# Two waits of TensorE for its own sums behind a layer norm, left out

## The chip, the cores and the metric

The kernel runs on one core of one Trainium2 chip. The metric is the device time of one execution in microseconds. Three runs of the kernel before took 1831.89, 1832.02 and 1832.16 us; the median is 1832.02 us.

## The reference, cut to what matters

One decoder block over 16 meta tokens and 256 tokens of width 2048, in float32: a half-step SwiGLU feed-forward (inner width 5632), a token mixer, a second half-step feed-forward and a last RMS norm. The mixer makes one input projection, runs a gated short convolution on one half of its channels and a 31-tap convolution with a layer norm on the other, and ends in one output projection:

```
y_sc = b_sc * causal_dwconv(c_sc * v_sc, conv_sc_w)
z = a_cf * sigmoid(g_cf)
z = causal_dwconv(z, conv_cf_w) + conv_cf_b
y_cf = silu(layernorm(z, ln_cf_g, ln_cf_b))      # mean and variance over 1024 channels
h = concatenate([y_sc, y_cf], -1) @ w_out
```

The layer norm takes its mean and variance over the channels. The channels lie on the 128 partitions in 8 tiles, so each of the two statistics needs a sum over the tiles (VectorE) and then a sum over the partitions (TensorE, a product with a matrix of ones).

## The kernel before, in words

Activations lie transposed, channels on partitions and tokens along the free axis. Every float32 operand is split into a high part (written by ScalarE) and a low part (written by VectorE), and each 128x128 weight tile makes three products: high times high (line 591), high times low (592) and low times high (593). The last stage uses lines 717 to 719 for the same three.

The weights come in 640 blocks of 512 KB, in an order written out by hand, the same on all engines. For each block SyncE starts the transfer into one of four raw buffers (line 446) once the low part of the block four before is made; ScalarE writes the high part (line 845) once the transfer has landed and TensorE has used the block four before; VectorE writes the low part (line 1135); TensorE waits for it (`start_block`) and makes the block's 24 products. The stages are gu1, down1, ag, cv, b, out_sc, out_cf, gu2 and down2. Each engine's queue is in order, and between blocks it has the other work of the stage.

The change lies in out_sc, the first half of the output projection: 4 groups of 4 blocks, counted b = 0 to 15, then out_cf with b = 16 to 31. Group 0 and 2 accumulate in PSUM banks 0 to 3, group 1 and 3 in banks 4 to 7, each in columns 0 to 255 of its banks. The layer norm runs in the shadow of these blocks:

- VectorE finishes the last taps of the convolution and the sum over the 8 tiles, and splits it into `sum_hi` and `sum_lo`.
- After block 6 TensorE sums them over the partitions, two products with a matrix of ones (lines 606 and 607), into columns 256 to 511 of bank 0: `layernorm_sums`.
- VectorE, after it has made the low part of block 8, waits for that sum, scales it (`ln_mu`, line 1446) and centres the 8 tiles; ScalarE squares them (line 998), VectorE adds the squares up (lines 1453 to 1457) and splits the sum (1150, 1152). Then comes the low part of block 11.
- After block 10 TensorE sums over the partitions again, into columns 256 to 511 of bank 4; VectorE reads it (line 1462), makes the reciprocal root, normalizes, and writes the low parts of the layer norm's output, which out_cf reads from block 16 on.

After each sum TensorE has two kinds of wait: one for the sum's own end (`ln_mean_done`, `ln_var_done`) right behind it, and, one block later (b = 7 and b = 11), one for VectorE's having read it (`ln_mu_set`, `ln_var`), before the next group begins in those banks. TensorE waits for its own end at four more places: behind the sums of the three RMS norms (`square_sums`), and before out_sc's first block, for the end of the stage b.

Of the kernel before, what the change touches and what calls it, by code (L numbers as in the profile page):

```python
# [39 lines left out]
def build(nc, x, meta_tokens, ffn1_norm, ffn1_w_gate, ffn1_w_up, ffn1_w_down, mix_norm, w_in, b_in,  # L40
# [45 lines left out]
    with ExitStack() as ctx:  # L86
# [3 lines left out]
        def sem(name):  # L90
            return ctx.enter_context(nc.semaphore(name))
# [205 lines left out]
        ln_mean_done, ln_mu_set, centred = sem("ln_mean_done"), sem("ln_mu_set"), sem("centred")  # L297
        ln_sq, ln_var_sum, ln_var_done = sem("ln_sq"), sem("ln_var_sum"), sem("ln_var_done")
# [27 lines left out]
        def banks_before(phase, g):  # L326

            return KD + SET * group0[phase] + SET * g
# [214 lines left out]
        def _(pe):  # L543
# [60 lines left out]
            def sum_over_partitions(dst, toks):  # L604

                pe.matmul(dst, ones_r[:, :], sum_hi[:, toks], start=True, stop=False)
                return pe.matmul(dst, ones_r[:, :], sum_lo[:, toks], start=False, stop=True)  # L607
# [189 lines left out]
            def layernorm_sums(b):  # L797


                if b == 6:  # L800
                    pe.wait_ge(sum_low, nth_sum["ln_mean"])
                    pe.wait_ge(emptied, banks_before("out_sc", 1))
                    sum_over_partitions(ps[:, 0, SEQ:2 * SEQ], slice(0, SEQ)).then_inc(ln_mean_done, 1)
                    pe.wait_ge(ln_mean_done, 1)
                if b == 10:
                    pe.wait_ge(sum_low, nth_sum["ln_var"])
                    pe.wait_ge(emptied, banks_before("out_sc", 2))
                    sum_over_partitions(ps[:, SET, SEQ:2 * SEQ], slice(0, SEQ)).then_inc(ln_var_done, 1)
                    pe.wait_ge(ln_var_done, 1)

                if b == 7:
                    pe.wait_ge(ln_mu_set, 1)
                if b == 11:
                    pe.wait_ge(ln_var, 1)
# [9 lines left out]
            for g in range(G_D):  # L824
                single_group("out_sc", g, g % 2, y_hi, y_lo, 0, slice(0, SEQ), KS,
                             ysc_lo, lambda i: i + 1, layernorm_sums)
# [840 lines left out]
```

## Time and profile before

| | |
|---|---|
| median of three runs | 1832.02 us |
| the profiled execution | 1831.56 us |
| its span | 1829.7 us |
| TensorE products busy | 1819.4 us, 99% |
| VectorE busy | 1190.7 us, 65% |
| ScalarE busy | 932.6 us, 51% |
| mean granted TensorE clock | 0.999 |

The span is the time from the first to the last instruction; 1831.56 - 1829.7 = 1.86 us of the profiled execution lie around it. PE is TensorE's products, PEld its weight loads, DVE is VectorE, ACT ScalarE, SP SyncE. Busy PE includes products that overlap, so 99% says that one product at least was under way. The chain of waits is followed backwards from the last instruction, at each step to what released it.

### The profile page before, as it was taken

What the parts mean: (1) busy time and instruction counts of PE and PEld (TensorE: products, weight loads), DVE (VectorE), ACT (ScalarE), POOL (GpSimd) and SP (SyncE); (2) the same over time, 40 slices, a digit from 0 to 9 for tenths busy, and PEclk for the clock granted to TensorE, in tenths of its full rate; (3) what the DMA queues carried; (4) which work ended last, traced back from release to release, by engine and by line L of the source; (5) the groups of instructions that cost most, each with busy time, mean ns of one, the idle gap of its engine ahead of it and who ended that gap; (6) DMA issues with size and microseconds to landing.
All of it is one profiled execution on the core that took longest, in us unless ns stands there. A gap on an engine that the chain in (4) does not pass through costs nothing.

```text
span 1829.7 us, 34627 instructions
## 1 busy us (share of the span) xinstructions
PE 1819.4 (99%) x14327; PEld 1778.0 (97%) x14327; DVE 1190.7 (65%) x1383; ACT 932.6 (51%) x1181; POOL 5.5 (0%) x15
## 2 busy tenths in 40 slices
PE   9999999999999999999999999999999999999998
PEld 9999999999999999999999999999999999988886
DVE  7555555555554544468899997755555565588897
ACT  7434343444433443349988776444444444455554
POOL 1000000000000000000000000000000000000000
PEclk9999999999999999999999999999999999999999
DMA  7655555555567777756556565966666666677665
GB/s 236 192 177 175 181 174 181 173 180 175 177 176 177 179 178 179 177 168 190 178 185 189 170 207 183 239 207 190 193 192 195 195 191 191 193 225 240 197 209 164
DMA packets 301845, 346.53 MB, mean 189 GB/s; under 512 B 27711, under 2 KB 241057, under 8 KB 301760
## 3 DMA queue, kind: packets, MB, share of 16 engines
q1 hardware_dynamic: 283104, 340.44, 62.1%
q10 hardware_dynamic: 18368, 4.73, 1.3%
q8 instruction: 58, 0.95, 0.2%
q14 instruction: 27, 0.22, 0.0%
q0 software_dynamic: 288, 0.19, 0.0%
HBM read 341.11 MB, written 4.19 MB: 189 GB/s over the span
## 4 chain that ended last, share of the span: by engine, by line
PE 98%; DVE 1%; ACT 0%; DMA 0%; issue 0%; SPq 0%; DVEq 0%; ACTq 0%
PE ps L591 29%; PE ps L593 29%; PE ps L592 29%; PE ps L718 4%; PE ps L717 4%; PE ps L719 4%; DMA m_rows<-in_meta_tokens 0%; DVE w_same__lo L1135 0%; PE ps L553 0%; DVE o_tok L1348 0%; ACT sq_tok L868 0%; DVE o_tok L1627 0%; DVE o_tok L1371 0%; DVE partial L1342 0%; PE ps L622 0%
## 5 line engine op out<-in xcount | busy, mean ns | idle before, releaser
L593 PE MATMUL ps<-x_hi,w_class__lo 128*128 128x272 f32 (+2 forms) x3200 | 901.6, 282 | 0.0
L591 PE MATMUL ps<-x_hi,w_class__hi 128*128 128x272 f32 (+2 forms) x3200 | 900.8, 281 | 0.1
L592 PE MATMUL ps<-x_lo,w_class__hi 128*128 128x272 f32 (+2 forms) x3200 | 900.3, 281 | 0.0
L1135 DVE TENSOR_TENSOR w_class__lo<-raw,w_class__hi 128x1024 fp32r<-128x1024 f32 x400 | 489.2, 1224 | 402.8 <-ACT w_class__hi L845 401.3
L845 ACT ACTIVATE w_class__hi<-raw 128x1024 fp32r<-128x1024 f32 x400 | 424.1, 1061 | 558.5 <-PE ps L593 558.2
L592 PEld LDWEIGHTS ps<-x_lo,w_class__hi 128*128 128x128 f32 x3200 | 602.2, 188 | 0.0
L591 PEld LDWEIGHTS ps<-x_hi,w_class__hi 128*128 128x128 f32 x3200 | 601.5, 188 | 0.3 <-PE ps L607 0.3
L593 PEld LDWEIGHTS ps<-x_hi,w_class__lo 128*128 128x128 f32 x3200 | 601.5, 188 | 0.0
L845 ACT ACTIVATE w_same__hi<-raw 128x1024 fp32r<-128x1024 f32 x200 | 210.9, 1059 | 261.0 <-PE ps L593 172.4
L1135 DVE TENSOR_TENSOR w_same__lo<-raw,w_same__hi 128x1024 fp32r<-128x1024 f32 x200 | 241.3, 1222 | 144.6 <-ACT w_same__hi L845 144.3
L593 PE MATMUL ps<-a_hi,w_same__lo 128*128 128x272 f32 x640 | 183.4, 287 | 0.0
L591 PE MATMUL ps<-a_hi,w_same__hi 128*128 128x272 f32 x640 | 183.4, 287 | 0.0
L592 PE MATMUL ps<-a_lo,w_same__hi 128*128 128x272 f32 x640 | 183.3, 286 | 0.0
L592 PEld LDWEIGHTS ps<-a_lo,w_same__hi 128*128 128x128 f32 x640 | 120.6, 188 | 0.0
L591 PEld LDWEIGHTS ps<-a_hi,w_same__hi 128*128 128x128 f32 x640 | 120.5, 188 | 0.0
L593 PEld LDWEIGHTS ps<-a_hi,w_same__lo 128*128 128x128 f32 x640 | 120.5, 188 | 0.0
L718 PE MATMUL ps<-w_same__hi,a_both 128*128 128x512 f32 x262 | 101.9, 389 | 0.0
L717 PE MATMUL ps<-w_same__hi,a_both 128*128 128x512 f32 x262 | 101.9, 389 | 0.0
L719 PE MATMUL ps<-w_same__lo,a_both 128*128 128x512 f32 x262 | 101.9, 389 | 0.0
L990 ACT ACTIVATE tap_product<-z,par 128x256 f32<-128x256 f32 x232 | 98.8, 494 | 0.0
L591 PE MATMUL ps<-y_both,w_same__hi 128*128 128x256 f32 x256 | 71.0, 277 | 0.2
L592 PE MATMUL ps<-y_both,w_same__hi 128*128 128x256 f32 x256 | 70.7, 276 | 0.0
(204 smaller groups left out, 1705.5 us busy)
## 6 DMA issues: line engine op xcount, KB each, us to landing
raw<-in_ffn_w_up SPq DMA_DIRECT2D x176, 512.0 KB, 3.5
raw<-in_ffn_w_down SPq DMA_DIRECT2D x176, 512.0 KB, 5.1
raw<-in_ffn_w_gate SPq DMA_DIRECT2D x175, 512.0 KB, 3.5
raw<-in_w_in SPq DMA_DIRECT2D x80, 512.0 KB, 3.6
raw<-in_w_out SPq DMA_DIRECT2D x32, 512.0 KB, 4.8
x_tok<-in_x SPq DMA_DIRECT2D x4, 512.0 KB, 7.8
out_y<-res ACTq DMA_DIRECT2D x32, 64.0 KB, 4.1
o_tok<-out_y ACTq DMA_DIRECT2D x8, 256.0 KB, 5.6
```

The lines of the kernel that those rows point to most:

```text
L591: pe.matmul(dst, w_high, act_high, start=first, stop=False)
L592: pe.matmul(dst, w_high, act_low, start=False, stop=False)
L593: return pe.matmul(dst, w_low, act_high, start=False, stop=last)
L717: pe.matmul(dst, act_high, w_high, start=begins, stop=False)
L718: pe.matmul(dst, act_low, w_high, start=False, stop=False)
L719: return pe.matmul(dst, act_high, w_low, start=False, stop=ends)
L845: act.activation(block_weights(phase, g, i)[0], raw_rows(phase, s), ACT.Copy).then_inc(hi_ready, 1)
L990: act.activation(tap_product[:, q % PRODUCTS, c % 2, :], z[:, c, 2 + n:2 + n + SEQ], ACT.Copy, scale=cf_tap(2 + n, c)).then_inc(cf_product, 1)
L1135: dve.tensor_tensor(w_lo, raw_rows(phase, s), w_hi.bitcast(F32), ALU.subtract).then_inc(lo_ready, 1)
```

## The change

TensorE's waits for the end of its own two sums are left out. Nothing else is changed: VectorE still waits on `ln_mean_done` and `ln_var_done` before it reads the sums, and TensorE still waits one block later until VectorE has read them.

```diff
@@ -801,12 +801,10 @@
                     pe.wait_ge(sum_low, nth_sum["ln_mean"])
                     pe.wait_ge(emptied, banks_before("out_sc", 1))
                     sum_over_partitions(ps[:, 0, SEQ:2 * SEQ], slice(0, SEQ)).then_inc(ln_mean_done, 1)
-                    pe.wait_ge(ln_mean_done, 1)
                 if b == 10:
                     pe.wait_ge(sum_low, nth_sum["ln_var"])
                     pe.wait_ge(emptied, banks_before("out_sc", 2))
                     sum_over_partitions(ps[:, SET, SEQ:2 * SEQ], slice(0, SEQ)).then_inc(ln_var_done, 1)
-                    pe.wait_ge(ln_var_done, 1)
```

## Rows read from the trace of the kernel before

**Rows 1.** The page, parts 1, 2 and 4: busy times, clock in tenths, chain by engine
```profile
PE 1819.4 (99%) x14327; PEld 1778.0 (97%) x14327; DVE 1190.7 (65%) x1383; ACT 932.6 (51%) x1181; POOL 5.5 (0%) x15
...
PEclk9999999999999999999999999999999999999999
...
PE 98%; DVE 1%; ACT 0%; DMA 0%; issue 0%; SPq 0%; DVEq 0%; ACTq 0%
```

**Rows 2.** The waits of the weight loads, whole run: line waited for, total, times, longest
```profile
PEld ps L591 <- PE ps L607: 1.3, 5, 0.3
...
PEld ps L591 <- PE ps L593: 0.3, 1, 0.3
```

**Rows 3.** Timeline of PE around the mean's sum: start us, duration, line, operands
```profile
1043.00 0.28 PE L591 MATMUL ps<-y_both,w_same__hi 128*128 128x256 f32 x1
...
1045.72 0.28 PE L606 MATMUL ps<-sum_hi,ones_r 128*128 128x256 f32 x1
1045.84 0.28 PE L607 MATMUL ps<-sum_lo,ones_r 128*128 128x256 f32 x1
1046.18 0.39 PE L591 MATMUL ps<-y_both,w_same__hi 128*128 128x256 f32 x1
1046.40 0.28 PE L592 MATMUL ps<-y_both,w_same__hi 128*128 128x256 f32 x1
...
1047.10 0.28 PE L592 MATMUL ps<-y_both,w_same__hi 128*128 128x256 f32 x1
```

**Rows 4.** Timeline of the weight loads around the mean's sum; idle before one in brackets
```profile
1045.72 0.19 PEld L607 LDWEIGHTS ps<-sum_lo,ones_r 128*128 128x128 f32 x1
1046.17 0.19 PEld L591 LDWEIGHTS ps<-y_both,w_same__hi 128*128 128x128 f32 x1 [0.26 <-PE ps L607]
```

**Rows 5.** Timeline of PE around the variance's sum
```profile
1057.31 0.28 PE L607 MATMUL ps<-sum_lo,ones_r 128*128 128x256 f32 x1
1057.64 0.39 PE L591 MATMUL ps<-y_both,w_same__hi 128*128 128x256 f32 x1
1057.87 0.28 PE L592 MATMUL ps<-y_both,w_same__hi 128*128 128x256 f32 x1
...
1058.57 0.28 PE L592 MATMUL ps<-y_both,w_same__hi 128*128 128x256 f32 x1
```

**Rows 6.** Timeline of PE where the stage out_sc begins
```profile
1026.21 0.28 PE L593 MATMUL ps<-x_hi,w_kept__lo 128*128 128x256 f32 x1
1026.55 0.39 PE L591 MATMUL ps<-y_both,w_same__hi 128*128 128x256 f32 x1
```

**Rows 7.** Timeline of DVE beside the two sums
```profile
1046.16 0.42 DVE L1446 TENSOR_SCALAR ln_mu<-ps 128x256 f32<-128x256 f32 x1 [2.18 <-PE ps L607]
...
1055.19 0.43 DVE L1152 TENSOR_TENSOR sum_lo<-ln_sum,sum_hi 128x256 fp32r<-128x256 f32 x1
1055.53 1.22 DVE L1135 TENSOR_TENSOR w_same__lo<-raw,w_same__hi 128x1024 fp32r<-128x1024 f32 x1
1057.62 0.42 DVE L1462 TENSOR_SCALAR step<-ps 128x256 f32<-128x256 f32 x1 [0.87 <-PE ps L607]
```

**Rows 8.** Timeline of DVE before out_cf's second block
```profile
1071.74 2.36 DVE L1135 TENSOR_TENSOR w_same__lo<-raw,w_same__hi 128x1024 fp32r<-128x1024 f32 x2
```

**Rows 9.** Timeline of PE where the second block of out_cf begins
```profile
1074.09 0.28 PE L591 MATMUL ps<-y_both,w_same__hi 128*128 128x256 f32 x1
```

**Rows 10.** The chain that ended last, its last stretch: start us, us, what
```profile
1804.94 0.24 PE ps L719
...
1805.20 0.02 ACT partial L915
```

**Rows 11.** Timeline of ACT near the end
```profile
1808.28 1.06 ACT L845 ACTIVATE w_same__hi<-raw 128x1024 fp32r<-128x1024 f32 x1 [0.58 <-DMA raw<-in_ffn_w_down]
```

**Rows 12.** Timeline of DVE near the end
```profile
1811.58 2.35 DVE L1135 TENSOR_TENSOR w_same__lo<-raw,w_same__hi 128x1024 fp32r<-128x1024 f32 x2
```

**Rows 13.** The weight tiles' transfers, 1040 to 1800 us: time to landing
```profile
DMA to landing us min/median/max: 3.3/4.2/7.7
```

## The prediction, made before the change was run

> **What bounds the kernel now.** I read four views. First the page: PE is busy 99% of a span of 1829.7 us, its granted clock is 0.9 or more of full speed in all 40 slices, and the chain that ended last is PE for 98% of the span [rows 1]. So nearly every nanosecond in which TensorE stands still is in the span, and VectorE and ScalarE matter only where they make it stand still. Second, the waits of the weight loads. Apart from the first 10 us there are two lines: five waits for line 607, 1.3 us in total, and one of 0.3 us for line 593 [rows 2]. The five are the sums over the partitions, each followed by a wait for its own end; the change removes two of them, so this view prices the idle time at 2 x 1.3 / 5 = 0.52 us. Third, the timeline around the two sums, because idle time is not the whole price (below). Fourth, the last stretch of the chain, to see whether a gain at 1046 us reaches the end.
>
> **The two waits, step by step.** The undisturbed spacing comes from block 6: its first product starts at 1043.00 and line 606, 24 products later, at 1045.72 [rows 3], so 2.72 / 24 = 0.113 us a product. Behind the sum's second product (1045.84) the next should start at 1045.95; it starts at 1046.18, lasts 0.39 instead of 0.28, and the one behind it starts 0.22 later, at 1046.40 [rows 3]. The weight load shows why: loads and products normally run side by side, one load ahead; here the load of block 7 stood idle for 0.26 us, until the sum had ended, and starts at 1046.17, with its product [rows 4]. So three things are paid: the end of the sum (0.34 - 0.113 = 0.23 us), one load that nothing hides (0.22 - 0.113 = 0.11 us), and slightly wide spacings for the next few products. Together: from line 607 at 1045.84 to the eighth product of block 7 at 1047.10 are 1.26 us for 8 spacings; 8 x 0.1133 = 0.907; the wait costs 0.35 us. At the variance: 1057.31 to 1058.57, again 1.26 us, again 0.35 [rows 5]. Of another kind of work the same wait costs the same: before out_sc TensorE waits for the end of line 593, with 1026.55 - 1026.21 = 0.34 us to the next product [rows 6].
>
> What comes back in their place? Block 7 and block 11 still wait for their low part. At an ordinary block border that wait shows no widening (1045.72 is one spacing behind block 6, and the two lines of [rows 2] are all the waits there are), so its cost is nothing when the low part is early. Block 7's is long made: VectorE had been idle for 2.18 us before 1046.16 [rows 7]. I charge 0. Block 11's is close. VectorE starts it at 1055.53 and ends at 1055.53 + 1.22 = 1056.75 [rows 7]. Its start can't move forward with TensorE: it lies behind work that began with reading the mean at 1046.16, and the mean's sum itself starts no earlier than before. TensorE comes to block 11 0.35 us earlier from the first wait, and doesn't stand behind the second: its product would be at 1057.31 + 0.11 - 0.35 = 1057.07, the load one spacing ahead at 1056.96. That is 0.2 us after 1056.75. A handover from VectorE to TensorE is not among the rows; the nearest is from TensorE to its own load, 1045.84 + 0.28 = 1046.12 to 1046.17, 0.05 us [rows 3, 4]. So it is ready at about 1056.80, 0.15 us in time. I charge 0, and keep 0.2 us as the upper bound (late by a little, and then a load that nothing hides, 0.11).
>
> Sum: 0.353 + 0.353 = 0.71 us gained, 0 lost. The bounds from the rows are 0.52 (the idle time of the view of waits alone) and 0.74 (both starts are rounded to 0.01 us, and the last widened spacings may reach a product further).
>
> **Does it reach the end?** The variance's sum comes 0.35 us earlier (its operands are ready at 1055.19 + 0.43 = 1055.62 [rows 7], TensorE gets there at 1056.84), so VectorE's work behind it moves by 0.35 and TensorE by 0.71: VectorE's lead over TensorE shrinks by 0.36. The least lead that I find there is at out_cf's second block: its low part is the first of two that start at 1071.74 and take 2.36 together, so done at 1072.9 [rows 8]; its first product starts at 1074.09, the load at 1073.98 [rows 9]. A lead of 1.1 us becomes 0.7: no wait. At the end the last PE piece of the chain is line 719 at 1804.94, and ScalarE takes over at 1805.20, released by it [rows 10]; from there VectorE and ScalarE set the time, all counted from that release. So the last 25 us move as a whole. The transfers also hang on VectorE's low parts and move along.
>
> The Trainium skill bears on the size. "TensorE: Matmul & The Clock Gate", section Single matmul latency, gives (398 + N) / 2.4 ns for a lone product at full clock, and section Back-to-back issue gap gives N / 2.4 + 2.5 for a streamed one. For N = 256 that is 272 ns against 109 ns. The trace has 0.28 and 0.113 us for these two, so it agrees; the difference, 0.163 us each, would make 0.33 us for the two waits, 1831.7 on the median. It leaves out the unhidden load and the way from the semaphore to the load, which the timeline shows; the row decides. The same page (Step-by-step, part 1) has the next weights loaded while a product runs: that speaks for the load's 0.11 us coming back.
>
> **The own time and the median.** The profiled execution took 1831.56 us: span 1829.7, and 1.86 around it. The sum makes that 1829.0 and 1830.85. It stood 0.46 below the median of the three runs, 1832.02, so runs differ by more than the effect does. On the median: 1832.02 - 0.71 = 1831.31, said as 1831.3 us. A measurement of this kernel can tell about 0.2% from no change, 3.7 us; the whole effect is 0.04%.
>
> **The rivals.**
> (a) The low part of block 11 takes the place of the second wait. For it: the 0.15 us lead just worked out. Against it: the lead is positive. It would give back 0.05 to 0.2 us: 1831.4 to 1831.5.
> (b) Only the end of the sum is saved, and the first load of the next block still lies bare. For it: block 7's load had its own wait in both cases. Against it: ordinary borders have that wait and show no bare load. Gain 2 x 0.23 = 0.46: 1831.56.
> (c) The gain is absorbed before the end, or the diff does nothing because what holds TensorE there is something else. For it: the last 25 us of the chain are not PE. Against it: they start from a PE release, and the weight loads have no wait for another engine behind the start [rows 2]. 1832.0.
> (d) Slower: a transfer near the end. The high part that starts at 1808.28 had waited 0.58 us for its transfer [rows 11]; it ends at 1809.34, and its low part starts on VectorE at 1811.58 [rows 12], in the very stretch that sets the end: a lead of 2.24 us. Transfers land after 4.2 us in the median and 7.7 at most [rows 13]. If the new times make this one meet other traffic and go from the one to the other, it is 3.5 late, VectorE waits 3.5 - 2.24 = 1.3, and the result is 1.3 - 0.7 = 0.6 above before: 1832.6. It decides from 2.24 + 0.71 = 2.95 us of delay on. Against it: the transfers move along with their consumers, so nothing new meets.
>
> **Chances.** Forecast 0.68, (a) 0.12, (b) 0.05, (c) 0.11, (d) 0.04. The range takes the forecast with (a), (b) and most of (c), and leaves room for the scatter between executions, of which the 0.46 us above is the measure: 1830.8 to 1832.1 us. Faster by over 0.2%, which needs 3.7 us, has no case here: 0.02. Slower by as much: 0.02. Within 0.2%: 0.96.
>
> **What would show it.** The waits of the weight loads have three for line 607, 0.8 us in total, instead of five. In the timeline line 607 of the mean is followed by a product of block 7 after 0.11 us that lasts 0.28, and the same at the variance. Line 607 of the variance starts 0.35 us earlier, the last PE piece of the chain 0.71 earlier, and the span is 1829.0. Rival (a) shows as an idle load behind the variance's sum that waits for line 1135; (b) as a 0.39 us product; (c) as a new wait later on. The prediction is wrong if the span is above 1829.4 or if TensorE's part before 1804 us has not moved by 0.6 to 0.8 us.

## The result: slower by 2.6 us, and the profile after

| | before | after |
|---|---|---|
| median of 20 runs each | 1831.88 us (1831.46 to 1832.70) | 1834.47 us (1833.87 to 1835.13) |
| ratio | | 1.0014, 95% interval 1.0008 to 1.0020 |
| the profiled execution, its span | 1831.56, 1829.7 us | 1834.84, 1833.0 us |

The change cost 2.6 us where 0.7 us of gain was predicted. It is small, but the interval leaves out no change. The two waits are gone from the waits of the weight loads, to which [rows 2] had five and one:

```profile
PEld ps L591 <- PE ps L607: 0.8, 3, 0.3
...
PEld ps L591 <- PE ps L593: 0.3, 1, 0.3
```

So is the gap behind the mean's sum, in the timeline of PE that answers to [rows 3]:

```profile
1046.62 0.28 PE L606 MATMUL ps<-sum_hi,ones_r 128*128 128x256 f32 x1
1046.74 0.28 PE L607 MATMUL ps<-sum_lo,ones_r 128*128 128x256 f32 x1
1046.86 0.28 PE L591 MATMUL ps<-y_both,w_same__hi 128*128 128x256 f32 x1
1046.98 0.28 PE L592 MATMUL ps<-y_both,w_same__hi 128*128 128x256 f32 x1
1047.09 0.28 PE L593 MATMUL ps<-y_both,w_same__lo 128*128 128x256 f32 x1
```

Line 607 is followed after 0.12 us, and the product behind it lasts 0.28 us, not 0.39. All of this was predicted. But look at the spacings: 0.12, 0.12, 0.11, where block 6 had 0.113. One block later it is plain; this row is 24 products behind 1046.86:

```profile
1049.68 0.28 PE L591 MATMUL ps<-y_both,w_same__hi 128*128 128x256 f32 x1
```

(1049.68 - 1046.86) / 24 = 0.1175 us a product. Taken over whole blocks, from the exact starts in the trace, the spacing is 113.3 ns in all of out_sc, out_cf and gu2 before, and 117.8 ns after, from block 7 of out_sc to block 3 of gu2. Then comes the sum of gu2's norm with its wait, which is left in, and the spacing is 113.3 again. The view of busy time by stretches shows it as a count of products. Its columns are: the stretch, its length, the busy time and in brackets the number of instructions of PE, PEld, DVE, ACT and POOL, the granted clock, the DMA share, GB/s. The number behind PE is the count. Four stretches: out_sc's blocks before the mean's sum; between the two sums; behind the variance's sum up to gu2's; gu2. The kernel before:

```profile
1032.00:1044.00 12.00, 12.00 (x108) 12.00 (x107) 11.84 (x19) 7.31 (x10) 0.00 (x0) 1.00 0.55 177
1048.00:1056.00 8.00, 8.00 (x73) 8.00 (x72) 7.86 (x13) 5.19 (x5) 0.00 (x0) 1.00 0.47 150
1062.00:1122.00 60.00, 60.00 (x532) 60.00 (x531) 53.23 (x91) 42.34 (x68) 0.00 (x0) 1.00 0.65 204
1140.00:1200.00 60.00, 60.00 (x531) 60.00 (x531) 40.59 (x44) 27.07 (x29) 0.00 (x0) 1.00 0.90 236
```

The kernel after:

```profile
1032.00:1044.00 12.00, 12.00 (x108) 12.00 (x107) 11.86 (x20) 7.47 (x12) 0.00 (x0) 1.00 0.51 166
1048.00:1056.00 8.00, 8.00 (x70) 8.00 (x69) 7.90 (x11) 4.33 (x4) 0.00 (x0) 1.00 0.46 154
1062.00:1122.00 60.00, 60.00 (x512) 60.00 (x511) 51.56 (x86) 40.59 (x67) 0.00 (x0) 1.00 0.64 201
1140.00:1200.00 60.00, 60.00 (x531) 60.00 (x531) 42.30 (x48) 28.36 (x30) 0.00 (x0) 1.00 0.87 228
```

The first and the last stretch have the same count within one; between the sums 70 stand against 73, behind them 512 against 532: 60 us / 532 = 0.113, 60 / 512 = 0.117 (a product counts if it overlaps the stretch, so each count is two or three high). The granted clock is 1.00 in all eight lines, and in the two slow stretches VectorE and ScalarE are no busier than before, but for 0.04 us of VectorE in the second. TensorE is at work all the time in every stretch.

One view does show the pace without counting: the mean time of one instruction, by line. In 1062 to 1122 us a product has 276 ns before and 281 after, whichever its line. Among the weight loads every third is longer, that of line 593 (the last number before the idle time is the mean in ns; before, then after):

```profile
L593 PEld LDWEIGHTS ps<-y_both,w_same__lo 128*128 128x128 f32 x156 | 29.3, 188 | 0.0
```

```profile
L593 PEld LDWEIGHTS ps<-y_both,w_same__lo 128*128 128x128 f32 x158 | 30.3, 192 | 0.0
```

The loads of the other two lines have 188 ns in both. From the stage b on this holds in every trace: one load of three is longer wherever the pace is slow, and none where it is fast.

The size follows: 29 blocks of 24 products at 117.78 - 113.33 = 4.45 ns make 3.10 us; less the 0.71 us of the two waits, 2.39. It can be measured between the same two instructions, out_sc's first product and line 607 in gu2. Before, the first is in [rows 6] and the second is this:

```profile
1125.89 0.28 PE L607 MATMUL ps<-sum_lo,ones_r 128*128 128x256 f32 x1
```

After, they are these two:

```profile
1027.45 0.39 PE L591 MATMUL ps<-y_both,w_same__hi 128*128 128x256 f32 x1
```

```profile
1129.17 0.28 PE L607 MATMUL ps<-sum_lo,ones_r 128*128 128x256 f32 x1
```

Before 1125.89 - 1026.55 [rows 6] = 99.34 us, after 1129.17 - 1027.45 = 101.72: 2.38 more. The other 0.90 us by which this profile is longer lie before out_sc (1027.45 against 1026.55), in the first 10 us, where three profiles of the unchanged kernel differ by 0.7 us too. The medians differ by 2.6; the 0.2 beyond 2.4 are within what the executions scatter.

### The profile page after: what moved, and what is told of

The parts are those of the page before. It is cut to its first block, busy times and chain, and to the rows that moved or that the text cites. A ratio compares the mean times of both kernels' runs of the same rounds, so it can differ in the third digit from the quotient of the medians.

```text
span 1833.0 us, 34625 instructions
## 1 busy us (share of the span) xinstructions
PE 1823.0 (99%) x14327; PEld 1782.1 (97%) x14327; DVE 1190.5 (65%) x1383; ACT 932.5 (51%) x1181; POOL 5.5 (0%) x15
## 4 chain that ended last, share of the span: by engine, by line
PE 98%; DVE 1%; ACT 0%; issue 0%; DVEq 0%; ACTq 0%
PE ps L593 29%; PE ps L591 29%; PE ps L592 29%; PE ps L717 4%; PE ps L718 4%; PE ps L719 4%; PE ps L573 0%; PE ps L553 0%; DVE w_same__lo L1133 0%; DVE o_tok L1346 0%; ACT sq_tok L866 0%; DVE o_tok L1625 0%; DVE o_tok L1369 0%; DVE partial L1340 0%; PE ps L622 0%
```

## The experiments

Sixteen runs were made. Three of them repeat the two main kernels (e5, e12, e16), and three repeat the kernel of another run (e6, e14, e15). Where nothing else is said the base is the changed kernel. "Slow pace" is 117.8 ns a product, "fast pace" 113.3. Each group of runs was timed beside the kernel before on one chip: e1 to e8 on one, e9 to e12 on a second, e13 to e16 on a third.

One thing has to be known before the traces are compared. There are two kinds of execution, and they part long before out_sc, in code that no run changed. In both, TensorE waits for its own end behind the sum of gu1's norm, at 33 us. The first product behind that wait, in the kernel before and in e2:

```profile
33.02 0.39 PE L591 MATMUL ps<-x_hi,w_rows_hi 128*128 128x272 f32 x1
```

```profile
33.73 0.40 PE L591 MATMUL ps<-x_hi,w_rows_hi 128*128 128x272 f32 x1
```

By the exact times it lasts 394 ns in the first kind, and the next one starts 230 ns behind it; in the second kind it is 397 and 233 to 234 ns. At the next such sum, at 807 us, each trace has its own two numbers again, and behind the wait before out_sc the next product starts after 229 to 230 ns in the first kind, 221 to 222 in the second. Each of the 18 traces is clearly one or the other. The first kind are the two main profiles and e1, e3, e5, e6, e10, e12, e13, e15 and e16; the second are e2, e4, e7, e8, e9, e11 and e14. Each chip had both. With y at its own place, out_sc begins fast in all traces of the first kind and slow in all of the second. What makes an execution of the one kind or the other isn't known; by 33 us it is settled. So what an edit does is read from traces of one kind.

**One wait put back, and a wait put elsewhere.**

```diff
# e1: behind the mean's sum
+                    pe.wait_ge(ln_mean_done, 1)
# e2 and e6: behind the variance's sum instead
+                    pe.wait_ge(ln_var_done, 1)
# e3: behind block 7, and likewise behind block 11
                 if b == 7:
+                    pe.wait_ge(block_used, block0["out_sc"] + 8)
                     pe.wait_ge(ln_mu_set, 1)
```

> The changed kernel with the wait behind the mean's sum put back; only the one behind the variance's sum stays out. Theory (pace): once the products of a sum run on without a wait, every product behind them is issued 117.8 ns after the one before instead of 113.3, until TensorE's next wait for its own end. Then blocks 7 to 10 of out_sc keep 113.3 ns, and the 25 blocks from b = 11 to the sum in gu2 (600 products) take 4.5 ns more each: +2.7 us, less 0.35 for the wait, so 2.3 us above before, about 1834.2 us. Rival (neighbours): the slower products come from reads and writes of VectorE, ScalarE and the transfers that TensorE now meets at other moments; they would depend on the times, not on which wait is gone, so with half the shift the slow stretch should be partly gone from both places and the time lie between, 1832 to 1833.

Stretches two and three of e1:

```profile
1048.00:1056.00 8.00, 8.00 (x73) 8.00 (x72) 7.86 (x13) 4.87 (x4) 0.00 (x0) 1.00 0.50 154
1062.00:1122.00 60.00, 60.00 (x512) 60.00 (x511) 51.60 (x88) 40.40 (x68) 0.00 (x0) 1.00 0.64 202
```

73 products between the sums, 512 behind the second: the fast pace where the wait is, the slow one from where it is missing. Time: 1.0012 of the kernel before, interval 1.0002 to 1.0021, medians 1835.26 against 1833.28, 2.0 us. The theory had 2.3, and 2.31 us is what lies between the two traces from out_sc's first block to gu2's sum (the medians may mix the two kinds of execution: the profiled one took 1834.21 us, the nine others 1835.08 to 1835.90); the rival, which wanted a time between and both stretches partly slow, is out.

> The changed kernel with a wait of TensorE for its own end one block later, behind blocks 7 and 11, where it already waits for VectorE's having read the sum. Theory (pace): any wait for the own end resets the pace, wherever it stands: 117.8 ns in block 7 and in block 11, 113.3 in all others; the span about 0.2 us above before's (2 x 24 x 4.5 ns; the two waits cost what they cost before). Rival (the sum must be drained before the next product): the pace stays at 117.8 behind the later waits, since the sums themselves still run on.

```profile
1048.00:1056.00 8.00, 7.94 (x69) 7.74 (x68) 7.86 (x13) 5.13 (x5) 0.00 (x0) 1.00 0.46 150
1062.00:1122.00 60.00, 60.00 (x532) 60.00 (x531) 53.13 (x92) 42.08 (x68) 0.00 (x0) 1.00 0.65 205
```

e3 has 532 products again behind the second late wait; by blocks only 7 and 11 are slow (117.7), 8 to 10 and all from 12 on fast. From out_sc's first product to line 607 in gu2 it takes 99.54 us against 99.34 before: the 0.2 us of the theory. In the second stretch lies the late wait itself. So the wait doesn't matter for what the sum computes: it restarts the stream, and one block later does as well.

> The changed kernel with the wait behind the variance's sum put back; only the one behind the mean's sum stays out. Theory (pace): 117.8 ns in the 4 blocks b = 7 to 10, 113.3 from b = 11 on: 96 x 4.5 ns = 0.43 us lost, 0.35 gained, the span about 0.1 us above before's. Rival (neighbours): no sharp border at the variance's wait; slow products also behind b = 11.

e2 failed the expectation at once: span 1851.8 us.

```profile
1032.00:1044.00 12.00, 12.00 (x105) 12.00 (x104) 11.86 (x19) 7.30 (x11) 0.00 (x0) 1.00 0.55 170
1048.00:1056.00 8.00, 8.00 (x73) 8.00 (x72) 7.90 (x11) 4.47 (x5) 0.00 (x0) 1.00 0.46 142
1062.00:1122.00 60.00, 60.00 (x512) 60.00 (x512) 51.13 (x84) 40.42 (x65) 0.00 (x0) 1.00 0.66 201
1140.00:1200.00 60.00, 60.00 (x512) 60.00 (x511) 41.55 (x48) 27.27 (x29) 0.00 (x0) 1.00 0.85 219
```

105 products in the first stretch: it was slow already before the sum, in code that is the same in all kernels. Behind the mean's sum, without a wait, it turned fast (73). Behind the variance's sum, with the wait, it turned slow (512), and stayed so through gu2, whose own wait did not help: the 172 blocks of gu2 behind its sum have 4128 products, at 4.45 ns 18.4 us. So a missing wait is not "slow" and a wait not "fast". It is an execution of the second kind. The load of 192 ns is that of line 591 up to the mean's sum and behind the variance's, and that of line 593 behind gu2's. In 1062 to 1122 us:

```profile
L591 PEld LDWEIGHTS ps<-y_both,w_same__hi 128*128 128x128 f32 x159 | 30.5, 192 | 0.0
```

The same kernel was run again.

> The kernel with the wait behind the variance's sum kept and the mean's left out, as before, timed in rounds. Theory (two paces, settled in the execution): its times scatter over several levels, from about 0.1 us above the kernel before (all fast but four blocks) to about 20 us above (gu2's 3840 products at 4.5 ns more are 17 us). Rival (the pace belongs to the program): every execution is about 20 us above.

```profile
1032.00:1044.00 12.00, 12.00 (x108) 12.00 (x107) 11.86 (x19) 7.31 (x12) 0.00 (x0) 1.00 0.56 164
1048.00:1056.00 8.00, 8.00 (x71) 8.00 (x70) 7.86 (x12) 4.76 (x4) 0.00 (x0) 1.00 0.45 153
1062.00:1122.00 60.00, 60.00 (x531) 60.00 (x531) 53.24 (x92) 42.47 (x69) 0.00 (x0) 1.00 0.65 208
```

The same program, in an execution of the first kind, and now as first expected: slow only between the sums, fast in gu2, span 1830.3. Its five executions took 1832.12, 1853.11, 1853.27, 1853.54 and 1853.86 us (1.0112 of before, 1.0093 to 1.0130). One program, two patterns, one for each kind of execution. That the four long ones were of e2's kind is argued from their times; they have no trace.

**Where the mean's products get their operands.** Each leaves the variance's wait in, so that what is read is the border between block 6 and block 7. All of them leave the mean out of the computation. Starts are given in bytes within 256: the matrix of ones starts at 128, `sum_hi` and `sum_lo` at 0 and 64, y (the block's moving operand) at 192, and the tile of y that serves as weights at 0, where the block's own weights start.

```diff
# e4 and e14: weights and moving operand from y (in a new ln_products, for the mean's sum alone)
-                pe.matmul(dst, ones_r[:, :], sum_hi[:, toks], start=True, stop=False)
-                return pe.matmul(dst, ones_r[:, :], sum_lo[:, toks], start=False, stop=True)
+                pe.matmul(dst, y_hi[:, 0, META:META + P], y_hi[:, 0, :], start=True, stop=False)
+                return pe.matmul(dst, y_hi[:, 0, META:META + P], y_hi[:, 1, :], start=False, stop=True)
# e9: ones_r with y moving; e10: y's tile as weights with sum_hi, sum_lo moving
# e13: the two products left out
```

> The changed kernel with the wait behind the variance's sum put back, and the mean's two products made from a tile of y, both as weights and as the moving operand, in the place of the matrix of ones and the split sum; so the mean is left out of the computation. Their operands then start at the same offsets within 256 bytes as a block's own. Theory (pace, set off by the operands' places): blocks 7 to 10 stay at 113.3 ns and the span is 0.35 to 0.4 us below before's. Rival (pace, set off by two further products, or by the change of the PSUM columns, whatever the operands): blocks 7 to 10 at 117.8 ns.

> The kernel with the mean's products made from y alone (weights and moving operand; the mean is left out of the computation), for a second profile. Theory (the operands' places set the pace off): block 7 has block 6's pace again; in an execution that starts out_sc at 113.3 ns it stays at 113.3. Rival (any two further products do it): 113.3 ns before the sum and 117.8 behind it.

> The changed kernel with the variance's wait put back, and the mean's two products made from the matrix of ones as weights and two tiles of y as the moving operand; the mean is left out of the computation. With both operands taken from y the pace did not change at the sum (117.8 ns before and behind it); with the sum's own operands it changed at it in all profiles so far, from 113.3 to 117.8 or back. Theory (the moving operand's place): the split sum starts at 0 and 64 within 256 bytes, y at 192, and it is this that shifts the reads in time; with y moving, block 7 of out_sc keeps the pace of block 6, whichever that is. Rival (the weights' place, 128 for the matrix of ones against 0): the pace changes between block 6 and block 7.

> The counterpart: a tile of y as weights, starting at 0 within 256 bytes as the block's own weights do, and the split sum as the moving operand; the mean is left out of the computation, the variance's wait is there. Theory (the moving operand's place): the pace changes between block 6 and block 7. Rival (the weights' place): it does not.

> The changed kernel with the variance's wait put back and the mean's two products left out altogether; VectorE scales what group 0 left in bank 0 instead, so the mean is left out of the computation. Theory (the sum's products set the pace off): block 7 of out_sc keeps the pace of block 6, 113.3 or 117.8 ns. Rival (something else at that place, such as the block border or VectorE's work that begins there): the pace changes between blocks 6 and 7 all the same.

Stretches one and two of e4, e9, e10 and e13, in this order:

```profile
1032.00:1044.00 12.00, 12.00 (x104) 12.00 (x103) 11.86 (x19) 6.76 (x10) 0.00 (x0) 1.00 0.58 171
1048.00:1056.00 8.00, 8.00 (x70) 8.00 (x69) 7.90 (x11) 4.32 (x4) 0.00 (x0) 1.00 0.43 144
```

```profile
1032.00:1044.00 12.00, 12.00 (x104) 12.00 (x103) 11.86 (x19) 6.99 (x10) 0.00 (x0) 1.00 0.56 172
1048.00:1056.00 8.00, 8.00 (x73) 8.00 (x72) 7.90 (x11) 4.48 (x5) 0.00 (x0) 1.00 0.48 139
```

```profile
1032.00:1044.00 12.00, 12.00 (x109) 12.00 (x108) 11.86 (x19) 7.32 (x12) 0.00 (x0) 1.00 0.54 171
1048.00:1056.00 8.00, 8.00 (x70) 8.00 (x69) 7.86 (x12) 4.72 (x4) 0.00 (x0) 1.00 0.49 160
```

```profile
1032.00:1044.00 12.00, 12.00 (x108) 12.00 (x107) 11.86 (x19) 7.31 (x12) 0.00 (x0) 1.00 0.59 169
1048.00:1056.00 8.00, 8.00 (x73) 8.00 (x72) 7.00 (x12) 4.70 (x5) 0.00 (x0) 1.00 0.47 161
```

Slow and slow; slow and fast; fast and slow; fast and fast. e14 repeats e4, slow and slow (span 1831.5 against 1830.7). e4, e14 and e9 are executions of the second kind, e10 and e13 of the first, so they can't be read as one row of four:

- First kind: fast before the sum. Without the two products it stays fast (e13). With the sum's own operands (e12, e6) and with weights from y and the sum moving (e10) it turns slow.
- Second kind: slow before the sum. With the sum's own operands (e2) and with the matrix of ones and y moving (e9) it turns fast. With both from y it stays slow (e4, e14). There the load of 192 ns goes from line 591 to line 592, as it must if every third one simply goes on being the long one through two further products.

The theory for e9, that the moving operand alone decides, fails in the second kind. In the first it holds so far: e10's rival (the weights) is out, and e15 below, whose sum has the places of e9's, stays fast. e9 then is as e2: slow behind the variance's wait and in all of gu2, span 1851.5.

**Other places for the operands.** By the assertions in the code, y and gu2's moving operand start at 192 within 256 bytes and their weights at 0. In the stage b the moving operand starts at 0, 64, 128 and 192 in turn, two blocks each, and the weights 64 further. Its blocks alternate: two at 113.3 to 113.5 ns, two at 117.7, in every profile. Before, blocks 8 and 9 of stage b (start 0) and blocks 10 and 11 (start 64) have these two stretches of 5 us:

```profile
1004.60:1009.60 5.00, 5.00 (x47) 5.00 (x46) 4.83 (x9) 3.53 (x6) 0.00 (x0) 1.00 0.37 105
1010.00:1015.00 5.00, 5.00 (x45) 5.00 (x44) 5.00 (x8) 5.00 (x11) 0.00 (x0) 1.00 0.64 169
```

```diff
# e7
-        mix_at = a_at + 0
+        mix_at = a_at + 64
-                both = w_class[0] if phase in ("cv", "gu2") else w_same[0]
+                both = w_class[0] if phase in ("cv", "gu2") else w_same[1]
# e8: besides, x2_hi and x2_lo (gu2's moving operand) 64 bytes further, weights w_class[1]
```

> The changed kernel (no waits behind the two sums) with all the mixer's tiles in the activation region 64 bytes further, so that y, the moving operand of out_sc and out_cf, starts at 0 instead of 192 within 256 bytes, and the weights of these stages at 64 instead of 0. In the stage b of the kernel before, products whose moving operand starts at 0 or 128 within 256 bytes go at 113.3 to 113.5 ns, those at 64 or 192 at 117.7. Theory (the operand's place decides whether a slow pace exists): out_sc and out_cf go at 113.3 ns throughout, without any wait, and the span is 0.7 us below that of the kernel before in its fast pattern, 1829.0. Rival (the sum's products leave a slow pace behind wherever the operands lie): 117.8 ns from block 7 of out_sc on.

> As the one before, and in gu2 too the moving operand starts 64 bytes further, at 0 within 256 bytes, and the weights at 64. Theory (place): out_sc, out_cf and gu2 at 113.3 ns in every execution; its times are narrow, 0.7 us below the fastest pattern of the kernel before, about 1831.2, whatever the kernel before shows beside it. Rival (the pace is settled at a wait, wherever the operands lie): some executions have 117.8 ns in gu2 and are 17 us longer.

The four stretches of e8:

```profile
1032.00:1044.00 12.00, 12.00 (x109) 12.00 (x108) 11.86 (x19) 7.32 (x11) 0.00 (x0) 1.00 0.53 172
1048.00:1056.00 8.00, 8.00 (x70) 8.00 (x69) 7.86 (x13) 5.12 (x5) 0.00 (x0) 1.00 0.46 154
1062.00:1122.00 60.00, 60.00 (x532) 60.00 (x531) 53.58 (x92) 42.33 (x68) 0.00 (x0) 1.00 0.65 206
1140.00:1200.00 60.00, 60.00 (x512) 60.00 (x511) 39.51 (x43) 26.18 (x30) 0.00 (x0) 1.00 0.90 228
```

This theory fell. With y at 0 the mean's sum made blocks 7 to 10 slow all the same, the variance's sum turned them back, and gu2 was slow from its own sum on: 1.0106 of before, interval 1.0088 to 1.0124. e7 had the same pattern in out_sc, but turned slow where gu2 begins, the border at which the moving operand's start goes back from 0 to 192, with no sum there. A place is not fast or slow by itself; a change of place can flip the pace, as in stage b. Both are executions of the second kind, so they can't be set beside the changed kernel's, which were of the first. In that kind y at 192 makes out_sc begin slow (e2, e4, e9, e11, e14) and y at 0 makes it begin fast (e7, e8).

**The sums at y's place.** e11 and e15 are one complete kernel: no waits, and the layer norm's split sums at 192 within 256 bytes.

```diff
+        ln_hi = at("ln_hi", sq_at + 192, [P, SEQ], F32R)
+        ln_lo = at("ln_lo", sq_at + 192 + 1280, [P, SEQ], F32R)
-                    sum_over_partitions(ps[:, 0, SEQ:2 * SEQ], slice(0, SEQ)).then_inc(ln_mean_done, 1)
+                    ln_products(ps[:, 0, SEQ:2 * SEQ]).then_inc(ln_mean_done, 1)
# ln_products: ones_r with ln_hi, then ln_lo; the same for the variance; VectorE splits into ln_hi, ln_lo
```

> The changed kernel, complete, without both waits, with the layer norm's split sums put where they start at 192 within 256 bytes, as y does; the matrix of ones stays at 128. Theory (the moving operand's place): the pace of out_sc's block 6 goes on through blocks 7 and 11 to the sum in gu2. If the execution is of the kind in which the kernel before goes at 113.3 ns, the time is 0.7 us below it. Rival (the weights' place): as the changed kernel, 117.8 ns from block 7 on, 2 to 3 us above before.

> The complete kernel without both waits, with the layer norm's split sums at 192 within 256 bytes, in five rounds. In its first profile out_sc went at 117.8 ns up to the mean's sum and at 113.3 from there to the end of gu2; it was 0.6 us below the kernel before in the median. Theory (the phase behind the variance's sum is now good in either kind of execution): again 0.3 to 1.2 us below before in the median, with less scatter than before's. Rival (that was luck of its ten executions): some executions 2 us or more above before.

Stretches one, two and three of e11, then of e15:

```profile
1032.00:1044.00 12.00, 12.00 (x105) 12.00 (x104) 11.71 (x19) 6.71 (x10) 0.00 (x0) 1.00 0.55 177
1048.00:1056.00 8.00, 8.00 (x73) 8.00 (x73) 7.86 (x12) 4.82 (x4) 0.00 (x0) 1.00 0.42 141
1062.00:1122.00 60.00, 60.00 (x532) 60.00 (x531) 53.47 (x92) 42.43 (x69) 0.00 (x0) 1.00 0.66 207
```

```profile
1032.00:1044.00 12.00, 12.00 (x109) 12.00 (x108) 11.86 (x19) 7.31 (x12) 0.00 (x0) 1.00 0.56 173
1048.00:1056.00 8.00, 8.00 (x73) 8.00 (x73) 7.86 (x12) 4.91 (x5) 0.00 (x0) 1.00 0.45 148
1062.00:1122.00 60.00, 60.00 (x532) 60.00 (x531) 53.49 (x92) 42.28 (x69) 0.00 (x0) 1.00 0.66 206
```

e11 began slow and turned fast at the mean's sum; e15 was fast from end to end. e11 is of the second kind, e15 of the first. So in the first kind the change of the sum's place does what it should: at the mean's sum e12 turns slow and e15 stays fast. In the second e11 turns fast at the mean's sum as e2 and e9 do, and behind the variance's sum, with no wait, it stays fast. The executions of both runs keep together, 1831.02 to 1831.89 and 1830.87 to 1831.94 us. Medians 1831.53 against 1832.12 of the kernel before beside it, and 1831.44 against 1832.02: 0.6 us below both times, but the ratios, 0.9996 with 0.9986 to 1.0005 and 0.9996 with 0.9987 to 1.0005, don't exclude no difference. Against the changed kernel, which ran beside e11 as e12, there is no doubt: its fastest run took 1833.87.

**The two kernels again.**

> The kernel before, unchanged, for a second profile. A fourth run left a question: with the variance's wait kept and the mean's left out, products went at 117.8 ns already in out_sc's first block, which the edit does not touch, and again in all of gu2. Theory (two paces): from a wait for its own end on TensorE runs on at one of two paces, 113.3 or 117.8 ns, and which one is settled at that wait and differs between executions. Then this profile may show another pattern than the first one, in out_sc or gu2. Rival (the pace belongs to the program): it shows 113.3 ns in out_sc, out_cf and gu2, as the first profile did.

> The changed kernel itself, for a second profile and for its times beside those of the kernel before on this chip. Theory (two paces, settled in the execution): either 113.3 ns up to block 6 of out_sc and 117.8 from block 7 to the sum in gu2, as in the first profile, 2.4 us above the kernel before at its fastest; or 117.8 ns up to block 6 and 113.3 behind the mean's sum. Rival (the pace belongs to the program): the first pattern, in every execution.

> The kernel before, unchanged, for a third profile. Theory (two kinds of execution): with even odds out_sc begins at 117.8 ns here, stays so up to one of the sums, and the span is 0.4 to 1.3 us above 1829.7; gu2 at 113.3. Rival (one pattern): 113.3 ns throughout, as twice before.

e5 and e16, the kernel before, are fast throughout (spans 1829.9 and 1830.4), as in the first profile. e12, the changed kernel, shows the first profile's pattern (108 to 109, 70, 512 and 532 products; span 1832.7) and is 1.0012 of before, 1.0003 to 1.0022. None of these three is of the second kind, and neither are the two main profiles. Seven of the sixteen runs' profiles are, all of other kernels; what the kernels before and after do in it has no trace. Beside e1 to e4 and beside e5 to e8 the kernel before had a median of 1833.28 and 1833.14 us, 1.2 us above the 1831.9 to 1832.1 elsewhere; out_sc's 11 blocks up to the variance's sum at the slow pace would cost 11 x 24 x 4.45 ns = 1.17 us. That those executions were of the second kind is argued, not shown: none of them has a trace, and those two groups are also the only ones of their chip, though e5 took 1831.72 us on it.

## Why the prediction was wrong, step by step

- **What bounds the kernel**: right. TensorE's stream sets the time, and its change came out at the end in full: line 607 in gu2 and the last product both come 3.28 us later than in the trace of before.
- **The price of a wait, 0.35 us, and the sum of 0.71**: right as a price. In e15, the one profile in which nothing else changed at the sums, out_sc's first product and the last of gu2's sum are at these places:

```profile
1027.08 0.39 PE L594 MATMUL ps<-y_both,w_same__hi 128*128 128x256 f32 x1
```

```profile
1125.69 0.28 PE L610 MATMUL ps<-sum_lo,ones_r 128*128 128x256 f32 x1
```

  1125.69 - 1027.08 = 98.61 us against 99.34 before, an execution of the same kind: 0.73 gained, where the working had 0.353 + 0.353.
- **"What comes back in their place?"**: this is the step that failed. It looked for another wait and, finding none, charged 0. What came back is no wait but a spacing: it took the 0.113 us of block 6 for the stream's own and let it go on behind the sum. Behind the sum without a wait it is 0.1178. 4.45 ns are invisible in one row of a timeline with two decimals, and 696 times 4.45 ns, 3.1 us, are four times the gain. One of the prediction's own signs shows it early: line 607 of the variance was to start 0.35 us earlier, and counted from out_sc's first product it starts 0.07 us later, for the 96 products between the sums lost 0.43.
- **It stood in the profile of before**: the two rows of stage b above, 47 against 45 products in 5 us. One kind of product had two paces there. The prediction priced a product from one block and did not ask whether that price holds elsewhere. Its "slightly wide spacings for the next few products" were a hint too: behind a wait the stream takes a few products to settle, and it took for granted what it settles at.
- **The low part of block 11 (rival a)**: no weight load waited for it. **The unhidden load (rival b)**: it is hidden again, as the forecast had it. **Absorbed (c)** and **the late transfer (d)**: neither; from 33 us to block 7, and again behind gu2's sum, every block keeps its distance in time from the other trace's to 0.002 us.
- **The side**: the slower rival, with 0.04, was the wrong mechanism. It looked among transfers and engines, never in TensorE's stream itself.

The Trainium skill, "TensorE: Matmul & The Clock Gate", section Back-to-back issue gap, gives N / 2.4 + 2.5 = 109 ns for N = 256. Neither 113.3 nor 117.8 is that. The section says itself that this is for products by themselves and that in a stream of loads and products both set the spacing; the prediction called the formula one for a streamed product and took 113 for agreeing with 109. That difference of 4% is as large as the one between the two paces, which no single figure has room for.

What is shown: the pace changes at the sums' products (first kind: e12 and e10 against e13) or where the moving operand's start changes (e7, stage b), and by how much. A wait for the own end restarts the stream. In the eleven traces of the first kind every such wait from out_sc on is followed by the fast pace; in the second kind the variance's wait is too in e4 and e14, but not in e2 and e9, and gu2's not in e2, e7, e8 and e9. Kernel and kind together fix the pattern in every case that was seen twice (before with e5 and e16, after with e12, e4 with e14). What stays open is why: what makes the two kinds, and what a product's operand starts have to do with the pace. One load in three is the long one in every slow stretch, and it is not the same one in every stretch. The program repeats itself every three products, so a shift against that period would fit; it was not measured by itself.

## What to carry to other kernels

A wait that costs 0.35 us in the profile may be what restarts an engine's stream at its better pace: before it is taken out, count the products in equal stretches on either side of it, or read the mean time of one (276 against 281 ns here), and compare stages that issue the same instruction. If two paces show up anywhere, multiply their difference by all products up to the next restart; that sum, not the idle time, is the stake. And where a foreign product goes into such a stream, try it with its moving operand at the place that the stream's own has: in e15 that kept the pace without the waits, and the trace shows the 0.7 us, though the medians, 0.6 us apart, don't exclude no difference from before. Last, before two traces are compared, look at the same instructions ahead of the edit: if they differ there, as in e2 and e6, the difference behind it is not the edit's alone.

## What the runs showed of the hardware that was not expected

One instruction form (128x128 weights, 256 columns, float32, granted clock 1.00) has two steady spacings, 113.3 and 117.8 ns, over thousands of products, and the slow one stands with VectorE busy for 99% of a stretch (e4, the first) as with 66% (e8, the last). In the slow one a product lasts 281 ns instead of 276 and every third weight load 192 instead of 188. The pace of 4128 products of gu2 was settled at one wait before them or earlier: 18 us, 1% of the kernel (e2, e8, e9).

One program gave 1832.12 us once and 1853.1 to 1853.9 five times (e2 and e6), while its two profiles have the same granted clock, 0.999. After the first 10 us they differ in the spacing of products alone: by 7 and 8 ns in all behind the waits at 33 and 807 us, and where one is slow and the other fast by 4.45 ns a product. A single run of such a kernel says little.
